# Two mixers and two feed-forward layers on one core: six column tiles of the first input projection move into the recurrence that follows it

## The reference, cut to what matters

```python
z = rmsnorm(h, mix_norm[j]) @ mix_w_in[j]
y_a = rwkv7_bidir(z[..., :RWKV_COLS], ...)
y_b = hyena_bidir(z[..., RWKV_COLS:], ...)
h = h + jnp.concatenate([y_a, y_b], axis=-1) @ mix_w_out[j]
...
def step(S, inp):
    r_t, w_t, k_t, v_t, kk_t, a_t = inp
    sa = jnp.einsum('dbhvk,dbhk->dbhv', S, kk_t)
    S = (S * w_t[..., None, :] - sa[..., :, None] * (kk_t * a_t)[..., None, :]
         + v_t[..., :, None] * k_t[..., None, :])
    return S, jnp.einsum('dbhvk,dbhk->dbhv', S, r_t)
```

## Time and profile before

| | us |
|---|---|
| median of three runs (2901.39 to 2903.89) | 2901.48 |
| the profiled execution | 2900.6 |
| its span | 2899.3 |
| PE busy in the span | 2831.5 (98%) |
| DVE busy | 1681.6 (58%) |
| ACT busy | 725.0 (25%) |

### The profile page before, as it was taken

How to read it: one execution, slowest core, us unless ns; L and a number is a source line. 1 busy time by engine, 2 the same in 40 slices (tenths; PEclk the granted TensorE clock), 3 DMA queues, 4 the chain that set the end, 5 groups by cost and what they waited for, 6 DMA issues and landing times.

```text
span 2899.3 us, 43530 instructions
## 1 busy us (share of the span) xinstructions
PE 2831.5 (98%) x17810; PEld 2361.6 (81%) x17810; DVE 1681.6 (58%) x3195; ACT 725.0 (25%) x1798; POOL 37.5 (1%) x60
## 2 busy tenths in 40 slices
PE   9988999999999999999999999999999999999999
PEld 7777899877999888888544478888888888766999
DVE  3576688554877577762226357774366663135554
ACT  1353342233441311100235321110111110234220
POOL 0000000020000000000000000000000000000000
PEclk9999999999999999999999999999999999999999
DMA  8300356653556555532222045543345423222444
GB/s 279 106 3 8 123 166 173 214 146 120 163 167 195 176 184 186 177 95 79 83 72 67 30 138 180 178 137 94 125 160 167 149 75 105 96 80 88 149 145 115
DMA packets 349225, 376.30 MB, mean 130 GB/s; under 512 B 7299, under 2 KB 302612, under 8 KB 348260
## 3 DMA queue, kind: packets, MB, share of 16 engines
q1 hardware_dynamic: 323748, 285.68, 32.2%
q10 hardware_dynamic: 23072, 82.52, 8.2%
q0 software_dynamic: 2208, 5.31, 0.9%
HBM read 372.44 MB, written 1.05 MB: 129 GB/s over the span
## 4 chain that ended last, share of the span: by engine, by line
PE 91%; DVE 5%; ACT 2%; issue 2%; ACTq 0%; DMA 0%; DVEq 0%
PE acc L134 78%; PE aux L134 12%; PE aux L2815 1%; DVE sb_big L1419 1%; DVE sb_work L1419 1%; DVE sb_work L1620 0%; ACT sb_xn L298 0%; PE aux L2266 0%; ACTq L1399 0%; ACT sb_rstd L288 0%; DMA sb_x<-xT 0%; ACT acc L1586 0%; ACT sb_rstd L290 0%; DVE sb_work L3044 0%; DVE sb_xn L276 0%
## 5 line engine op out<-in xcount | busy, mean ns | idle before, releaser
L134 PE MATMUL acc<-sb_xn,weights 128*128 128x256 f32 (+3 forms) x4480 | 1002.7, 377 | 10.6 <-DVE sb_xn L276 6.4
L134 PEld LDWEIGHTS acc<-sb_xn,weights 128*128 128x128 f32 (+1 forms) x4480 | 765.4, 190 | 208.8 <-issue 123.8
L134 PE MATMUL acc<-sb_work 128*128 128x256 f32 (+1 forms) x1880 | 361.1, 346 | 0.0
L134 PEld LDWEIGHTS acc<-sb_work 128*128 128x128 f32 x1880 | 313.0, 191 | 33.3 <-issue 0.5
L134 PE MATMUL acc<-sb_work,weights 128*128 128x256 f32 (+2 forms) x1636 | 335.7, 353 | 1.4 <-DVE sb_work L1328 1.4
L134 PE MATMUL acc<-sb_big,weights 128*128 128x256 f32 (+1 forms) x1776 | 311.6, 333 | 8.1 <-ACT acc L1575 5.2
L134 PEld LDWEIGHTS acc<-sb_big,weights 128*128 128x128 f32 x1776 | 276.9, 191 | 36.9 <-ACT acc L1575 7.0
L134 PEld LDWEIGHTS acc<-sb_work,weights 128*128 128x128 f32 x1636 | 268.3, 191 | 46.8 <-issue 20.6
L134 PE MATMUL acc<-sb_xn,sb_work 128*128 128x256 f32 (+1 forms) x1200 | 231.7, 342 | 0.0
L134 PEld LDWEIGHTS acc<-sb_xn,sb_work 128*128 128x128 f32 x1200 | 196.9, 191 | 19.7
L1419 DVE SCALAR_TENSOR_TENSOR sb_work<-sb_work 128x1024 f32<-128x1024 f32 x128 | 156.5, 1223 | 2.8
(11 more groups left out here) (390 smaller groups left out, 3104.3 us busy)
## 6 DMA issues: line engine op xcount, KB each, us to landing
weights<-ffn_w_up SPq DMA_DIRECT2D x88, 1024.0 KB, 8.1
sb_work<-w_mod_rows ACTq DMA_DIRECT2D x134, 512.0 KB, 5.9
weights<-ffn_w_down SPq DMA_DIRECT2D x48, 1408.0 KB, 7.2
weights<-ffn_w_gate SPq DMA_DIRECT2D x44, 1024.0 KB, 5.5
weights<-mix_w_in SPq DMA_DIRECT2D x5, 2048.0 KB, 12.9
weights<-ple_w_gate SPq DMA_DIRECT2D x4, 2048.0 KB, 8.6
weights<-na_w_qkv SPq DMA_DIRECT2D x8, 1024.0 KB, 8.0
weights<-w_in SPq DMA_DIRECT2D x4, 2048.0 KB, 8.2
```

Source lines behind the costliest of these rows:

```text
L134: return te.matmul(o, lhsT, rhs, start=start, stop=stop, skip_group_check=True)
```

## The change

- `mix_in` holds 20 column tiles instead of 26: tiles 0 and 1 of r, of k and of v, the decay and rate inputs, the gate, and the Hyena columns. The loads are cut to match: r and k 256 columns each, then one block with two loads of 256 columns (v, and the inputs of decay, rate and gate).
- The filter steps, transforms and transposes are put behind other tiles: step 0 behind tile 1, 1 behind 3, 2 behind 5, then `7: (3, 4), 8: (5, 6), 9: (7,), ... 13: (11,)`; transforms behind tiles 14 to 17, transposes behind 17.
- The six tiles 2 and 3 of k, v and r (`late_tiles`) are computed by a generator, `tensor_late`, one product at a time, into banks 2 and 3 in turn; `fill(between, n)` takes n of its 48 products. They are taken at these places: 1 each ahead of the low-rank steps 2, 4 and 6 and 5 behind the last, in place of the 10 idle products; 12 ahead of the first pass, in place of the 24 idle ones; and in each of the first two passes 4 ahead of level 1, 2 each ahead of levels 3 and 5 and of the product with the inverse, 1 behind the local outputs, 3 at the end.
- ACT makes both copies of a late tile (`scalar_late`): tiles 0 and 1 of the list ahead of the first pass, 2, 3 and 5 behind the first copies of passes 0, 1 and 2, 4 at the end of pass 1.
- The normalised x is kept in `x[:, :, 0:CTX]`, where the context will lie, and the context's load moves from the middle of the projection's loads to behind the last late tile. On SP's queue two late loads come behind the Hyena blocks, then the output projection, then the wait for the last late tile, then the context and the first feed-forward block.

```diff
+    late_tiles = ((1, 2), (2, 2), (0, 2), (1, 3), (0, 3), (2, 3))
+    late_blocks = [open_block(loads=2), open_block()]
+    late = [(part, ct, next_group(late_blocks[part == 0], bank=2 + n % 2)) for n, (part, ct) in enumerate(late_tiles)]
...
+    def tensor_late():
+        for part, ct, g in late:
+            blk = late_blocks[part == 0][1]
+            te.wait_ge(weights_in[blk.slot].sem, blk.arrived_at)
+            te.wait_ge(acc_free[g.bank].sem, g.free_at)
+            t, c = k_tiles(blk.slot, 2048 if part == 2 else 0, KT, 256), 128 * (ct - 2)
+            for k in range(KT):
+                ins_ = mm(acc[g.bank][:, 0:L], t(k, c, c + 128), xm[:, k, :], k == 0, k == KT - 1)
+                if k == KT - 1:
+                    acc_full.on(ins_)
+                yield
...
+    def scalar_late(n):
+        part, ct, g = late[n]
+        at, ps = 8 * part + ct, acc[g.bank][:, 0:L]
+        ac.wait_ge(acc_full.sem, g.done_at)
+        zr_copied.on(ac.copy(zr[:, at, 1:L + 1], ps))
+        acc_free[g.bank].on(ac.copy(zr[:, at + 4, 1:L + 1], ps[:, ::-1]))
...
             else:
+                if n in (2, 4, 6):
+                    fill(between, 1)
                 te.wait_ge(lora_read.sem, lora_read_at(n - 2))
...
-        te.wait_ge(acc_free[2].sem, scan_banks[2])
-        tensor_idle(10, acc[2])
+        fill(between, 5)
...
         for lv in range(1, 6):
             n = 5 * p + lv - 1
+            if p < 2 and lv in (1, 3, 5):
+                fill(between, 4 if lv == 1 else 2)
             te.wait_ge(sc_xi.sem, sc_xi_at(n))
...
-        tensor_idle(24, acc[2])
+        fill(between, 12)
...
-        ctx_in.on(sp.dma_start(x[:, :, 0:CTX], ins["ctxT"].rearrange("(k p) t -> p k t", p=128)))
-        sync_wide(mix_in[5:], ins["mix_w_in"][0])
-        sync_wide(mix_out, ins["mix_w_out"][0])
+        sync_mix_in(mix_in[4:])
+        sync_late()
+        sync_wide(mix_out, ins["mix_w_out"][0])
+        sp.wait_ge(acc_full.sem, late[-1][2].done_at)
+        ctx_in.on(sp.dma_start(x[:, :, 0:CTX], ins["ctxT"].rearrange("(k p) t -> p k t", p=128)))
```

More of the change, by code:

```diff
@@ L385, in build @@
     filt_ready_at = filt_ready.reserve(4)
-    FILTER_STEP = {n: i for i, n in enumerate((2, 5, 8, 10, 11, 12, 13, 14, 15, 16, 17, 18))}
+    FILTER_STEPS = {1: (0,), 3: (1,), 5: (2,), 7: (3, 4), 8: (5, 6), 9: (7,), 10: (8,), 11: (9,), 12: (10,), 13: (11,)}
     def tensor_filter(i):
@@ L475, in tensor_mix_in @@
         group = 0
-        for blk, at, n in mix_in:
+        for blk, parts, n in mix_in:
             te.wait_ge(weights_in[blk.slot].sem, blk.arrived_at)
-            t = k_tiles(blk.slot, 0, KT, n)
             for i, g in enumerate(blk.groups):
-                tensor_group(g, [(t(k, 128 * i, 128 * i + 128), xv_l[:, k, :]) for k in range(KT)],
+                part, c = divmod(128 * i, n)
+                t = k_tiles(blk.slot, KT * n * part, KT, n)
+                tensor_group(g, [(t(k, c, c + 128), xm[:, k, :]) for k in range(KT)],
@@ L481, in tensor_mix_in @@
                              mix_norm.ready if group == 0 else None)
[L482 to L486, removed]
+                for step in FILTER_STEPS.get(group, ()):
+                    tensor_filter(step)
+                if 14 <= group < 18:
+                    tensor_transform(group - 14)
+                if group == 17:
@@ L487, in tensor_mix_in, with sync_mix_in, sync_late @@
                     tensor_by_time()
                 group += 1
+    def sync_mix_in(plan):
+        wv = ins["mix_w_in"][0].rearrange("(k p) n -> p k n", p=128)
+        for blk, parts, n in plan:
+            sync_load(blk, [(slots[blk.slot][:, KT * n * i:KT * n * (i + 1)].rearrange("p (k n) -> p k n", k=KT), wv[:, :, at:at + n])
+                            for i, at in enumerate(parts)])
+    def sync_late():
+        (_, kv), (_, r) = late_blocks
+        sync_mix_in([(kv, (C + 256, 2 * C + 256), 256), (r, (256,), 256)])
@@ L490, in vector_mix_in, with fill @@
+    def fill(products, n):
+        for _ in range(n):
+            next(products)
+    def scalar_late(n):
[4 more added lines that the diff above has]
+        acc_free[g.bank].on(ac.copy(zr[:, at + 4, 1:L + 1], ps[:, ::-1]))
     def vector_mix_in():
@@ L492, in vector_mix_in @@
         for n, g in enumerate(mix_groups):
-            if n in FILTER_STEP:
-                vector_filter(FILTER_STEP[n])
-            if n == 20:
+            for step in FILTER_STEPS.get(n, ()):
+                vector_filter(step)
+            if n == 14:
                 vector_lora()
-            elif n == 24:
+            elif n == 18:
                 ve.wait_ge(hy_t.sem, hy_t_at(0))
@@ L517, in scalar_mix_in @@
         for n, g in enumerate(mix_groups):
-            if n in FILTER_STEP:
-                scalar_filter(FILTER_STEP[n])
-            if n == 19:
+            for step in FILTER_STEPS.get(n, ()):
+                scalar_filter(step)
+            if n == 14:
                 scalar_gate_input()
-            elif 20 <= n < 24:
-                scalar_transform(n - 20)
-            elif n == 24:
+            elif 15 <= n < 19:
+                scalar_transform(n - 15)
+            if n == 18:
                 ac.wait_ge(hy_t.sem, hy_t_at(0))
                 hy_tm.on(ac.copy(s_tm[:, 0, :], aux[0][:]))
-            if n == 22:
+            if n == 17:
                 ac.wait_ge(wad_set.sem, wad_set_at(1))
@@ L675, in tensor_gate, with tensor_lora @@
             gate.on(ins_)
-    def tensor_lora(first):
+    def tensor_lora(first, between):
         te.wait_ge(wad_tanh.sem, wad_tanh_at(0))
@@ L715, in build @@
     b0, b1 = acc[0], acc[1]
-    scan_banks = [acc_free[b].planned for b in range(3)]
+    scan_banks = [acc_free[b].planned for b in range(2)]
     NP = CT
@@ L915, in shares @@
                 (pd_set if g else a_step).on(ac.activation(dst[:, g, :], zr[:, at, 0:L], ACT.Copy, scale=cols("mu", 1, at)))
+        if p >= 2:
+            ac.wait_ge(zr_copied.sem, zr_at(3 * p + 3))
+            for *_, g in late[3 * p - 5:3 * p - 3]:
+                ac.wait_ge(acc_free[g.bank].sem, g.freed_at)
         shares(t1, 8)
@@ L977, in build, with tensor_scan @@
     BY_IDENT = (3, 4)
-    def tensor_scan(p, ahead):
+    def tensor_scan(p, ahead, between):
         def times(out_bank, lhs, rhs_, start=None):
@@ L1053, in tensor_scan @@
                 next(ahead, None)
+        if p < 2:
+            fill(between, 2)
         te.wait_ge(sc_xu.sem, sc_xu_at(5 * p + 4))
@@ L1114, in tensor_scan @@
                 sc_y.on(local_out((b0, b1), 1))
+        if p < 2:
+            fill(between, 3)
     def scalar_scan(p, ahead):
@@ L1227, in vector_scan, with tensor_recurrence @@
                                  quads((b0, b1)[par][:, 256:512]).rearrange("p (g a) t -> p g a t", g=2), ALU.add))
-    def tensor_recurrence(first):
+    def tensor_recurrence(first, between):
         for _ in first:
             pass
-        tensor_idle(24, acc[2])
+        fill(between, 12)
         for p in range(NP):
-            tensor_scan(p, tensor_ahead(p + 1) if p + 1 < NP else iter(()))
+            tensor_scan(p, tensor_ahead(p + 1) if p + 1 < NP else iter(()), between)
         tensor_scan_out(NP - 1)
@@ L1240, in scalar_recurrence @@
             pass
+        scalar_late(0)
+        scalar_late(1)
         for p in range(NP):
@@ L3105, in tensor_program @@
         tensor_hyena()
-        first = tensor_prepare()
-        tensor_lora(first)
-        tensor_recurrence(first)
+        first, between = tensor_prepare(), tensor_late()
+        tensor_lora(first, between)
+        tensor_recurrence(first, between)
         tensor_mix_out()
```

39 lines of the change are left out of this document (21 added, 18 removed).

## The result

| | before | after |
|---|---|---|
| median of four runs | 2902.68 us (2901.39 to 2904.73) | 2882.04 us (2880.42 to 2885.48) |
| ratio, 95% interval | | 0.993 (0.9913 to 0.9947) |
| profiled execution, its span | 2900.60, 2899.3 us | 2882.26, 2881.0 us |

The changed kernel is faster by 0.7%, at 2882.0 us where 2881.7 was forecast. The page of the profile hardly shows it: PE has 68 instructions fewer and is still busy in 98% of the span.

The account below looks back on a forecast made before the run. PE was taken to bound the projection, a chain of small PE, ACT and DVE steps the passes; -21.0 + 0.3 + 0.1 + 2.1 - 1.3 = -19.8 us gave 2881.7 us at the median, range 2878 to 2887.

Parts of the forecast that it names:

- rival (3): Products in the first two passes are not hidden in the pauses: 15.2 us instead of 2.1, 2894.8 us; 7%.
- Six tiles, -21.0: Input projection: six column tiles removed at 3.50 us each save 21.0 us, ends -20.7 and -21.1.
- Tables, +0.3: Projection: the first filter step needs its tables sooner and may wait for their load, +0.3 us, ends 0 and 3.5.
- rival (2): Tables are late: PE stands at the first filter step up to 22.80 us, +3.2 us, 2884.9 us; 8%.
- Between projection and first pass, +0.1: Idle products give way to 8 and 12 real ones ahead of the first pass, +0.1 us, ends -0.3 and +0.5.
- Inside the first two passes, +2.1: 14 products in each pass cost only what overruns the pauses, +2.1 us together; upper end 15.2.
- a detour of 0.26: In the passes: going from 64x64 products to the full array and back costs 0.26 us beyond the products.
- The clock, -1.3: First pass: four products fill the pause behind which the granted clock fell, -1.3 us, ends -1.3 and 0.
- The loads, "no term": SP's queue: first feed-forward weights, issued later behind the last late product, still arrive before they are read; no cost.
- Rival (1): The clock falls at another pause in the shifted stretch: one fall more, 1.3 us, 2883.0 us; 10%.
- Rival (4): Slower: the granted clock stays low over the first two passes, kernel 18 us slower, 2920 us; 3%.

Follow-up runs that it names:

- the first experiment: Changed kernel with all 28 products of the first two passes put ahead of the first pass; 2893.63 us, ratio to the kernel before 0.9964.
- the last experiment: Changed kernel with context and first feed-forward loads behind the last pass, and one product moved from ahead of the first pass into its first pause; 2879.71 us, ratio 0.9919.

## Why the prediction was right

The mechanism is the one that was named: products taken out of the projection are worth their length, and most of it is hidden in the pauses. The experiments on the products exclude rival (3): 12.09 us ahead of the passes, 2.6 inside them. That the total was forecast within 0.3 us of the median is partly luck: a projection and a stretch ahead of the passes that were better by 0.8 and 0.3 made up for a third pass that was worse by 1.0 and a first product that came 0.2 later, and the runs of the changed kernel alone lie 5 us apart. Term by term:

- **Six tiles, -21.0.** Measured -21.51. In the chain of waits, from the first product to the first transform, the products alone account for 21.13. The other 0.38 come from the filter steps, which the prediction had looked at only for whether they would be late: in the chain of before, four places of 1.05 us with two instructions each (the first at 52.80 us); now two places of 1.91 us with four each.

```profile
42.67 1.91 PE aux L134 x4
44.58 3.65 PE acc L134 x16
48.23 1.91 PE aux L134 x4
```

- **Tables, +0.3.** Nothing. The first filter step stands directly behind two tiles, with no idle time in brackets, so rival (2) did not happen. The projection as a whole was 0.8 better than forecast, this 0.3 among it.

```profile
12.50 7.14 PE L134 MATMUL acc<-sb_x,weights 128*128 128x256 f32 x32
19.57 0.64 PE L134 MATMUL aux<-sb_work 17*64 17x256 f32 x2
```

- **Between projection and first pass, +0.1.** Measured -0.18, inside the ends. 12 products took 5.27 us against the 24 idle ones' 5.52, and the pass began as they ended.
- **Inside the first two passes, +2.1.** Measured 1.25 + 1.35 = 2.6. Set against the clean second pass of the first experiment, the places went over by 0.14 ahead of level 1 (forecast 0.16), 0.19 ahead of level 3 (0.15), 0.30 ahead of level 5 (0.25), 0.20 ahead of the inverse (0.15), 0.22 at the carried states (0.19) and 0.29 at the end (0.26). The method (pause, less products, less a detour of 0.26) gave every place to within 0.05; they add up to 1.34 where 1.16 was forecast. (The instructions from which the prediction took the detour are one product of 512 columns, not two; the 0.86 us of streaming are right.) The Trainium skill (TensorEngine Tiling (Array Packing), Key Properties) says that a change of tiling mode drains TensorE, without a figure. No row shows a drain by itself, but the rows agree in that a detour costs more than its products stream, by 0.26 us in the earlier trace rows. The first pass went over by 1.25, not by the 1.0 forecast; its first pause had room, as the last experiment shows, so the difference lies in the same small places. The second pass came out at the forecast +1.2 in the table because that of before has 0.19 us near its end that undisturbed passes (32.47 to 32.49) lack.
- **The clock, -1.3.** By itself 1.52, shown by the idle products in the kernel before; in the other direction 1.50 by leaving the pause open. The prediction had it too small mostly by the same 0.19, since it took the second pass of before as undisturbed; that the first pass met its forecast of -0.3 is this and its larger overrun, one against the other. The pause of 2.2 us in the first pass is what dropped the clock: it fell behind it in all three profiles that have this pause (the kernel before, all products ahead, the pause open), and in none of the six in which it is filled.
- **The loads, "no term".** This is the step that failed. The prediction asked whether the weights would arrive in time, which they did, and not what their burst does to whatever runs beside it. They cost 1.03 us of the third pass in the first profile and 1.30 in the second, of which 0.68 and 0.95 are the stop on issue. The kernel before loads nothing there, and with the loads behind the last pass the third pass was back at 32.48.

Rival (1), the clock at another pause, did not come in the third or fourth pass, where it was put, but 560 us into the span, at 1.6 us, close to its price of 1.3. The changed kernel's second profile is without it, so the change does not decide it. The Trainium skill (TensorE: Matmul & The Clock Gate, Part 1) was cited for a monitor that runs freely. The nine profiles agree with it, though they don't show it: one and the same pair of pauses, 1.77 and 1.62 us in each of them and behind the same code, dropped the clock in five of them and not in the other four. What decides it among these stays open. Rival (4) fell: the clock was 1.00 throughout both passes, in every profile in which the first pause was filled.

The first feed-forward came 19.52 us earlier, against a sum of -19.8. Of the gains beyond the forecast (0.8 in the projection, 0.3 ahead of the first pass), the third pass took back 1.0 and the later first product 0.23; the fall of the clock is what the one profile then lost on top.

## What to carry to other kernels

Work taken from a stage that PE bounds is worth its full length; put into pauses of a stage with a chain of small steps it costs only what it goes over, and a table of pause, products and detour forecasts that place by place. Fill first the pause that drops the clock, since that pays twice. When a change moves a load, ask not only whether it arrives in time but also what runs while it comes: here the burst was best put behind the passes, into the output projection, where it cost nothing.

## What the runs showed of the hardware

- A burst of 5 MB at about 355 GB/s stopped PE for 0.68 to 0.95 us in the middle of a row of small products, without any wait that the profile knows; the stop moved when the loads did, and was absent when they came behind the passes. It stood in front of the same instruction in three profiles, and PE went on 1.36 to 1.42 us after a packet of the instruction queue that had come late (with all products ahead, the burst made no such stop).
- The same code behind the same pause kept the clock in some executions and not in others, 560 us and 1600 us into the span, at up to 5 us together. Runs of one kernel differ by that much, and single runs should be compared by stage, up to a point ahead of it.
- Eight idle products in one pause of the kernel before gave back 1.5 us: extra work on the busiest engine made the pass shorter.
